# A two-layer diffusion transformer on one NeuronCore: how the end of layer two puts the residual, the last expert product and the final norm together

## The reference, cut to what matters

```python
def grouped_moe(h, router_w, router_bias, w1, w3, w2):
    ...
    for e in range(N_EXPERTS):
        he = (jax.nn.silu(h @ w1[e]) * (h @ w3[e])) @ w2[e]
        out = out + combine[:, e:e + 1] * he
    return out
...
        y = grouped_moe(tokens, router_w, router_bias, w1[l], w3[l], w2[l])
        x = x + mod[:, 5, None] * y[:B * S].reshape(B, S, D)
...
    return rmsnorm(x, g_final)     # x * rsqrt(mean(x*x) + EPS) * g_final
```

## Time and profile before

| | us |
|---|---|
| median of 3 runs | 1107.58 |
| lowest and highest run | 1102.73, 1112.13 |
| the profiled execution: span from the first to the last instruction | 1110.9 |

### The profile page before, as it was taken

The page is one execution under the profiler, slowest core; times in us unless marked ns, Lnnn a source line. Parts: engine busy times, 40 slices in busy tenths (PEclk is TensorE's granted clock), DMA queues, the critical chain, the costliest instruction groups (busy, mean ns, idle before and its releaser), DMA issues.

```text
span 1110.9 us, 24073 instructions
## 1 busy us (share of the span) xinstructions
PE 938.8 (85%) x9092; PEld 539.8 (49%) x9092; DVE 487.4 (44%) x1186; ACT 245.9 (22%) x485; POOL 192.7 (17%) x325
## 2 busy tenths in 40 slices
PE   3999999979986489999978699999798579967695
PEld 2536445555445255656634366543545335544353
DVE  2179336465664434443433576406642612221233
ACT  2100112343322122222222031113421112111121
POOL 4100000110020134443433320000100111110011
PEclk9999999999998689999988899999998689998898
DMA  9997612780003979999999998317802999999993
GB/s 344 396 398 269 263 73 76 216 362 1 1 1 148 379 297 398 418 413 412 414 415 403 369 357 335 110 44 260 335 1 95 374 368 418 412 401 420 410 416 149
DMA packets 58208, 315.75 MB, mean 284 GB/s; under 512 B 6909, under 2 KB 12229, under 8 KB 39169
## 3 DMA queue, kind: packets, MB, share of 16 engines
q1 hardware_dynamic: 47776, 292.17, 66.0%
q0 software_dynamic: 8336, 17.71, 4.4%
q10 hardware_dynamic: 2000, 4.47, 1.0%
HBM read 308.42 MB, written 11.60 MB: 288 GB/s over the span
## 4 chain that ended last, share of the span: by engine, by line
PE 53%; DMA 33%; DVE 5%; issue 4%; DVEq 2%; ACT 1%; SPq 1%; POOL 1%; ACTq 0%; POOLq 0%
PE ps L2011 49%; DMA ring<-in_w 17%; DMA area<-in_w 7%; DMA HT<-in_w 3%; DMA ring<-in_w_in 2%; DMA cst<-in_w 2%; PE ps L2295 2%; DMA area<-in_cst 1%; DMA XG<-in_w 1%; PE ps L2141 1%; DMA area<-h_rows,area 1%; DMA expert_rows<-area 1%; PE ps L2120 1%; PE ps L2320 0%; PE ps L2331 0%
## 5 line engine op out<-in xcount | busy, mean ns | idle before, releaser
L2011 PE MATMUL ps<-ring,area 128*32 128x256 f32 x3520 | 217.8, 400 | 45.9 <-issue 19.6
L2011 PE MATMUL ps<-ring,HT 128*128 128x512 f32 (+1 forms) x576 | 253.0, 591 | 2.3 <-issue 1.8
L2011 PE MATMUL ps<-area 128*32 128x256 f32 (+6 forms) x2072 | 179.4, 396 | 20.1 <-DVE area L1857 10.1
L2011 PEld LDWEIGHTS ps<-ring,area 128*32 128x32 f32 x3520 | 125.0, 115 | 135.2 <-issue 57.3
L2011 PEld LDWEIGHTS ps<-ring,HT 128*128 128x128 f32 x576 | 108.0, 193 | 126.1 <-issue 123.8
L2011 PEld LDWEIGHTS ps<-area 128*32 128x32 f32 (+4 forms) x2072 | 107.6, 147 | 70.0 <-issue 37.7
L1903 DVE STREAM_TRANSPOSE area<-area 128x256 f32<-128x256 f32 x63 | 28.1, 446 | 180.6 <-PE ps L2011 171.2
L2011 PE MATMUL ps<-HT,ring 128*128 128x256 f32 (+1 forms) x320 | 87.6, 432 | 3.5 <-DMA ring<-in_w_in 3.4
L994 POOL DMA_INDIRECT area<-h_rows,area x66 | 69.8, 1057 | 105.4 <-DVEq L1875 43.1
L2011 PEld LDWEIGHTS ps<-HT,ring 128*128 128x128 f32 x320 | 60.8, 193 | 24.9 <-issue 15.0
L1463 DVE SCALAR_TENSOR_TENSOR area<-area,CW 128x512 f32<-128x512 f32 (+1 forms) x120 | 68.8, 614 | 4.5 <-issue 0.5
(11 more groups left out here) (248 smaller groups left out, 900.6 us busy)
## 6 DMA issues: line engine op xcount, KB each, us to landing
ring<-in_w SPq DMA_DIRECT2D x56, 2048.0 KB
ring<-in_w_ada SPq DMA_DIRECT2D x24, 2048.0 KB
ring<-in_w_in SPq DMA_DIRECT2D x10, 2048.0 KB
area<-in_w SPq DMA_DIRECT2D x20, 1024.0 KB
HT<-in_w SPq DMA_DIRECT2D x8, 2048.0 KB
area<-in_w SPq DMA_DIRECT2D x8, 2048.0 KB
late<-in_w SPq DMA_DIRECT2D x8, 1536.0 KB
ring<-in_w_out SPq DMA_DIRECT2D x4, 2048.0 KB
```

The lines of the kernel that those rows point to most:

```text
L2011: return t_.matmul(out, lhsT, rhs, start=first, stop=last_)
```

## The change

It has four parts. First, in layer two PE adds the residual X into the sum banks right after it zeroes them: eight matmuls of the identity with X, one for each tile and column quarter. Second, the last down product goes into bank 1 (`B_END`), is issued before `add_rows(b)`, waits only for `gT`, and both `add_rows` follow it; its rows and one-hot have buffers of their own. Third, in every DVE step, in both layers, `gT` is made before `ym` and `oht`, as soon as the wait for the former down product has passed. Fourth, the end works by halves of the columns: ACT squares the sum banks directly (banks 0 and 1 of the sums, then 2 and 3, two tiles each), DVE meanwhile multiplies the other half with g_final into X, POOL puts the two half sums together and makes both tiles' roots in one go, then DVE scales tile 0 and half of tile 1, ACT the other half, and three stores follow.

```diff
@@ -546,6 +546,8 @@
         YL = cut(TILES * D, U7_AT).rearrange("p (t d) -> p t d", t=TILES)
         YA = [YL[:, 0], YL[:, 1], gate[:, 0], gate[:, 1]]
         YB = [YL[:, 2], YL[:, 3], area[:, 7 * D // 2:9 * D // 2], area[:, HTR_AT + D:HTR_AT + 2 * D]]
+        oht_end, ym_end = G0[0], ym[:, NW:2 * NW]
+        B_END = 1
         GFIN = area[:, AW - NW - D:AW - NW]
         G4 = area[:, AW - NW:AW]
         SQ = [area[:, c:c + D] for c in range(HTR_AT, HTR_AT + TILES * D, D)]
@@ -864,7 +866,9 @@
                         if n != ahead or k:
                             sp.dma_start(piece, src[:, row:row + piece.shape[1]]).then_inc(ring_full[x], 16)
                         row += piece.shape[1]
-            sp.wait_ge(fin_o, 3)
+            sp.wait_ge(fin_o, 1)
+            sp.dma_start(out_v[:, 0], X[:, 0]).then_inc(stored, 16)
+            sp.wait_ge(fin_o, 2)
             sp.dma_start(out_v[:, 1, 0:D // 2], X[:, 1, 0:D // 2]).then_inc(stored, 16)
 
 
@@ -1016,9 +1020,12 @@
                         for r in range(2):
                             gather(2 * i + r, r, pool.snap(made) + r)
                         pool.reg_add(made, made, 2)
-                    for i in range(nq):
-                        pool.wait_ge(ss_done, TILES * (l + 1) + i + 1)
-                        rsqrt(rstd[:, i:i + 1], ss[:, i:i + 1], ms[:, i:i + 1], D).then_inc(rs_done, 1)
+                    pool.wait_ge(ss_done, TILES * DEPTH + 1)
+                    link(g.tensor_scalar(ms[:, 2:4], ss[:, 0:2], 1.0 / D, EPS, ALU.mult, ALU.add))
+                    pool.wait_ge(ss_done, TILES * DEPTH + 2)
+                    link(g.tensor_scalar(ms[:, 0:2], ss[:, 2:4], 1.0 / D, None, ALU.mult))
+                    link(g.tensor_tensor(ms[:, 0:2], ms[:, 0:2], ms[:, 2:4], ALU.add))
+                    g.tensor_tensor(rstd[:, 0:2], ms[:, 0:2], half[:].to_broadcast([P, 2]), ALU.pow).then_inc(rs_done, 1)
                     barrier(pool, bar(l, 6))
                     return
                 pool.wait_ge(y_zero, 64)
@@ -1257,11 +1264,17 @@
                     with act.Fori(0, blocks) as b:
                         act.wait_ge(w13_full[l], b + 1)
                         s.activation(sg, ps[:, B_W13, 0:P], ACT.Silu).then_inc(si_rdy[l], 1)
-                    for i in range(2):
-                        third(l, i)
-                    act.wait_ge(fin_o, 2)
-                    act.dma_start(out_v[:, 0], X[:, 0]).then_inc(stored, 16)
-                    act.wait_ge(fin_o, 4)
+                    act.wait_ge(sums_full, l + 1)
+                    for h in range(2):
+                        if h == 1:
+                            act.wait_ge(comb[l], 1)
+                        for i in range(2):
+                            last = s.activation(SQ[i][:, h * CHUNK:(h + 1) * CHUNK].rearrange("p (j n) -> p j n", j=2), ps[:, B_SUM + 2 * h:B_SUM + 2 * h + 2, i * NW:(i + 1) * NW], ACT.Square,
+                                                accum_out=ss[:, 2 * h + i:2 * h + i + 1])
+                        last.then_inc(ss_done, 1)
+                    act.wait_ge(rs_done, TILES * DEPTH + 1)
+                    s.activation(X[:, 1, CHUNK:D], X[:, 1, CHUNK:D], ACT.Identity, scale=rstd[:, 1:2]).then_inc(comb[l], 1)
+                    act.wait_ge(comb[l], 3)
                     act.dma_start(out_v[:, 1, D // 2:D], X[:, 1, D // 2:D]).then_inc(stored, 16)
                     act.wait_ge(stored, 48)
                     barrier(act, bar(l, 6))
@@ -1914,7 +1927,7 @@
                     v.tensor_copy(xs, xg[:, bass.ds(at_, NW)])
                     dve.drain().then_inc(xs_rdy[l], 1)
 
-                def copy_y(m, summed=False):
+                def product_made(m):
 
                     if l < DEPTH - 1:
                         v.tensor_scalar(gb, G0[0], of_cond[0][:, bass.ds(m, 1)], None, ALU.mult)
@@ -1922,6 +1935,16 @@
                         v.scalar_tensor_tensor(gb, G0[1], of_cond[1][:, bass.ds(m, 1)], gb, ALU.mult, ALU.add)
                         dve.drain()
                     hold(dve, w2_full[l], m + 1, dve_passed)
+
+                def last_rows(m):
+
+                    v.tensor_scalar(oht_end, ROWS1, TK[:, bass.ds(m, 1)], None, ALU.is_equal)
+                    hold(dve, w2_full[l], m + 1, dve_passed)
+                    v.tensor_tensor(ym_end, ps[:, B_END, 0:NW], G4, ALU.mult)
+                    dve.drain().then_inc(y_rdy[l], 1)
+
+                def copy_y(m, summed=False):
+
                     if l == DEPTH - 1:
                         v.tensor_scalar(oht, ROWS1, TK[:, bass.ds(m, 1)], None, ALU.is_equal)
                         v.tensor_tensor(ym[:, 0:NW], ps[:, B_W2, 0:NW], G4, ALU.mult)
@@ -1948,9 +1971,11 @@
                     hold(dve, si_rdy[l], b + 1, dve_passed)
                     v.scalar_tensor_tensor(gg, sg, TW[:, bass.ds(b, 1)], ps[:, B_W13, P:2 * P], ALU.mult, ALU.mult).then_inc(g_rdy[l], 1)
                     if not isinstance(b, int) or b:
-                        copy_y(b - 1 if m is None else m, m is not None)
+                        product_made(b - 1 if m is None else m)
                     dve.drain()
                     v.transpose(gT, gg).then_inc(gt_rdy[l], 1)
+                    if not isinstance(b, int) or b:
+                        copy_y(b - 1 if m is None else m, m is not None)
                     copy_x(b + 2)
 
                 wait_made(dve, ("x0", l))
@@ -1976,18 +2001,25 @@
                     with dve.Fori(PEEL, blocks) as b:
                         step(b)
                         dve.reg_add(copied, copied, 1)
-                copy_y(dve.snap(copied), l < DEPTH - 1)
                 if l == DEPTH - 1:
+                    last_rows(dve.snap(copied))
+                    dve.wait_ge(fin_g, 16)
                     dve.wait_ge(sums_full, l + 1)
-                    for i in range(nq):
-                        add_sums(l, i)
-                    dve.wait_ge(fin_g, 16)
-                    for i in range(2):
-                        dve.wait_ge(rs_done, TILES * DEPTH + i + 1)
-                        for half in (slice(0, D // 2), slice(D // 2, D)):
-                            v.scalar_tensor_tensor(X[:, i, half], X[:, i, half], rstd[:, i:i + 1], GFIN[:, half], ALU.mult, ALU.mult).then_inc(fin_o, 1)
+                    for h in (1, 0):
+                        if h == 0:
+                            dve.wait_ge(ss_done, TILES * DEPTH + 1)
+                        cols = slice(h * CHUNK, (h + 1) * CHUNK)
+                        v.tensor_tensor(X[:, 0:2, cols].rearrange("p i (j n) -> p i j n", j=2),
+                                        ps[:, B_SUM + 2 * h:B_SUM + 2 * h + 2, :].rearrange("p j (i n) -> p i j n", i=2),
+                                        GFIN[:, cols].rearrange("p (j n) -> p j n", j=2).unsqueeze(1).to_broadcast([P, 2, 2, NW]), ALU.mult)
+                        dve.drain().then_inc(comb[l], 1)
+                    dve.wait_ge(rs_done, TILES * DEPTH + 1)
+                    v.tensor_scalar(X[:, 0], X[:, 0], rstd[:, 0:1], None, ALU.mult).then_inc(fin_o, 1)
+                    v.tensor_scalar(X[:, 1, 0:CHUNK], X[:, 1, 0:CHUNK], rstd[:, 1:2], None, ALU.mult).then_inc(fin_o, 1)
                     barrier(dve, bar(l, 6))
                     return
+                product_made(dve.snap(copied))
+                copy_y(dve.snap(copied), True)
                 dve.drain().then_inc(y_rdy[l], 1)
                 dve.drain().then_inc(phase, 1)
                 for i in range(2):
@@ -2379,7 +2411,10 @@
                 for j in range(NG):
                     claim(pe, ("sum", l, j))
                     rows = slice(SLOT * j, SLOT * (j + 1))
-                    made(mm(ps[:, B_SUM + j], cst[rows, C_ZERO:C_ZERO + P], cst[rows, C_I16:C_I16 + CHUNK], True, False), ("sum", l, j))
+                    last = mm(ps[:, B_SUM + j], cst[rows, C_ZERO:C_ZERO + P], cst[rows, C_I16:C_I16 + CHUNK], True, False)
+                    for i in range(S_LAT // P if l == DEPTH - 1 else 0):
+                        last = mm(ps[:, B_SUM + j, i * NW:(i + 1) * NW], ident, X[:, i, j * NW:(j + 1) * NW], False, False)
+                    made(last, ("sum", l, j))
 
                 def add_rows(b, stop=False):
 
@@ -2387,23 +2422,28 @@
                     for i in range(S_LAT // P):
                         for j in range(NG):
                             rows = slice(SLOT * j, SLOT * (j + 1))
-                            last = mm(ps[:, B_SUM + j, i * NW:(i + 1) * NW], oht[rows, i * P:(i + 1) * P], (ymx if l < DEPTH - 1 else ym)[rows, 0:NW], False, stop and i == S_LAT // P - 1)
+                            if l == DEPTH - 1:
+                                lhsT, rhs = (oht_end, ym_end) if stop else (oht, ym[:, 0:NW])
+                            else:
+                                lhsT, rhs = oht, ymx
+                            last = mm(ps[:, B_SUM + j, i * NW:(i + 1) * NW], lhsT[rows, i * P:(i + 1) * P], rhs[rows], False, stop and i == S_LAT // P - 1)
```

(16 more changed lines are left out.)

## The result

The changed kernel takes 1116.64 us in the median (1104.91 to 1125.67, 11 runs), the kernel before 1110.51 in the same comparison (1102.73 to 1114.52, 11 runs): ratio 1.0069, 95% interval 1.0041 to 1.0097. The ratio is the recorded one of the comparison and not the quotient of the two medians, which lie 6.1 us apart; the run of 1125.67 belongs to the slow state and is left out of it. By the ratio the change costs about 7.7 us (4.5 to 10.8), where 0.6 us of gain was forecast. The profiled execution took 1119.82 us with a span of 1117.9; the kernel before had 1110.9.

What follows compares the result with a forecast made beforehand. Layer two's experts were taken as bound by the weight stream, then PE's backlog, then a relay of single steps. Terms -1.4 (end), +0.4 (residual) and +0.4 (gT order) gave -0.6, so 1107.0 us from 1107.58; range 1102 to 1112.

Steps and rivals of the forecast that it cites:

- the residual on PE: Start of layer two's experts: residual matmuls take 3.5 us at full clock, unit 11 issued 2.9 later, cost 0.4 us.
- a sign of being wrong: Start of layer two's sums: residual records at 0.43 us each would show the prediction wrong; 0.22 was expected.
- rival A: Weight stream of layer two: the whole 2.9 us lag passes to the weights, total +1.9, 1109.5 us; chance 0.2.
- rival D: Start of layer two or loops: banks make an engine wait or reordering uncovers one; 1113 us or more; chance 0.05.
- The product tail: End of layer two, last down product and both add_rows: sums there 1.6 us earlier, bounds 0.6 to 2.4.
- the sum's 5.0 us: Product tail: forecast time from the end of the former down product to the end of the last add_rows.
- Rival C: Product tail: DVE late, PE waits 1 us; POOL takes another 0.5; tail -0.1, total +0.7, 1108.3; chance 0.15.
- the norm: End of layer two, from the sums to the first store: 5.15 us against 4.97, bounds 4.3 and 5.9.
- From the sums to the first store: End of layer two, squares, POOL's root and scaling: 5.15 us against 4.97, a loss of 0.2.
- Store to end: End of the kernel: 4.56 us kept, set by the first store's start plus the time of 1 MB.
- gT ahead of ym: DVE steps in both layers: rows come one transpose later, costing 0.4 us at the end of layer one.
- rival B: Start of layer two's experts: PE's clock stays up, the lag vanishes; -1.0, or -1.8 and 1105.8 us; chance 0.15.

Runs made afterwards that it cites:

- the grouped kernel: The changed kernel with the four zeroing matmuls first, then the eight residual matmuls; 1108.96 us, ratio 0.9973 to the kernel before.
- the kernel before, padded: The kernel before with only 64 semaphore increments added ahead of the routing matmuls, where PE is idle; one run, no ratio, product tail 11.3 us.
- the grouped, padded kernel: The changed kernel with zeroing first, residual after, plus 64 semaphore increments ahead of the routing matmuls; 1107.54 us, ratio 0.9965 to the kernel before.

## Why the prediction was wrong

The step that failed is the residual on PE: "Zeroing and residual are 2.1 + 7.0 us of work at 1.2 GHz; 2.1 of it is done by 886.3, the remaining 7.0 takes 3.5 at 2.4". Both halves of it are wrong for the code as it stands. The 2.1 us of zeroing is the time of four matmuls side by side, each on 32 rows of its own; alternated with matmuls over all rows, each takes 2.0. And the clock was taken from the kernel before, where it rose near 886.3; it doesn't rise here. Zeroing and residual took 16.0 us at 1.2 GHz, half of it each, where 5.6 was reckoned; a record of the residual took 0.50, beyond the 0.43 named as a sign of being wrong. Unit 11 came 14.5 us later and not 2.9: 14.0 by the start of the sums, 1.4 by the first up product at the lower clock (5.23 for 3.83), less 0.9 by PE's shorter pause behind it (1.25 for 2.16). With the matmuls grouped, the step's numbers came out nearly (2.09 and 3.82, unit 11 issued 2.7 us later where 2.9 was reckoned, stream full), so the price of the residual was right within 0.3 us and its arrangement, which I had read only for the number of matmuls, was not. That the clock rises late is shown; why it does stays open.

The rest of that part carried: SP waits for that home, the weight stream has no slack, and the loss is the distance of two issues less what is in flight, (904.05 - 887.32) - 5.1 = 11.6 us by the formula, 10.8 by the landing. That is rival A, to which I gave 0.2 and 2.9 us; its bound of 6.4 took half clock but not the zeroing. The median lies where I had put rival D, but what D named, a bank that makes an engine wait or a wait in the loop, isn't what the runs show.

The product tail was right in its mechanism and gained 0.5 instead of 1.6, since a load of code, which the kernel before hid behind its second wait for DVE, became the last to come. It appears in the earlier trace rows only as 2.04 for 32 records instead of 1.93. With the border moved the sum's 5.0 us is what was measured, by two errors of some 0.4 us that cancel. Rival C had PE wait 1 us again, which is near the 1.2 us between the 28th and the 29th record; its cause (DVE late) was wrong, as DVE had the rows ready in time, and its 0.5 us for POOL didn't come. Two sums of this part were also wrong as written: its bounds of 0.6 to 2.4 us of gain and of 4.3 to 5.9 us for the norm add up to +0.3 and -3.1, not to -0.1 and -2.6, and C's own parts make +0.1 for the tail, not -0.1. Neither reaches the size of the miss.

From the sums to the first store I had 5.15 and measured 4.95: POOL's three operations and hand-overs took 1.3 (root of two columns 0.73, estimate 0.72). Store to end 4.56, measured 4.57, as the end set by the first store and 1 MB would have it.

gT ahead of ym was forecast to cost 0.4 at the end of layer one and gained 0.45. Between the down product and DVE's first operation on the rows it was 1.37 us, and is now 0.93 with the transpose inside. In the code, waits for the scatters stand there; that the transpose now runs beside them is my reading and is not shown by itself. The clock of rival B: in the grouped kernel the fall is spared, as the Trainium skill's "TensorE: Matmul & The Clock Gate", Part 1, would have it; in the changed kernel PE was busy for 19 us at 1.2 GHz before it rose, which the same rule, read by busy time, doesn't foresee. The added work need not be the reason for what was spared: in the kernel before, padded, without any residual, the second up product came after 1.93 us of pause and took 3.66 as well.

## What to carry to other kernels

Matmuls on 32 rows each were cheap here only while they stood next to one another: before one puts anything between such matmuls, price each by itself. When a stream of weights bounds a stage, as here, look first at the PE work that stands ahead of a release that the stream's queue waits for; find that release and compare the distance of the two issues with what is in flight. And behind a loop with a length known only on the chip, the first work after the exit can wait for code at a place that any edit ahead of it moves, so a tail's gain has to be looked for again after each edit.

## What the runs showed of the hardware

Four fp32 zeroing matmuls (32 rows, 512 columns) took 2.09 us together on four different groups of rows, 7.19 on the same group, and 2.0 each between full-height ones, all at 1.2 GHz. The Trainium skill, "TensorEngine Tiling (Array Packing)", "The Solution" and "Theoretical Speedup", puts a factor of up to 4 on tiles of 32 rows; the trace agrees, with 3.4.

The granted clock stayed at 1.2 GHz for 19 us in which PE was busy all the time with such single matmuls, with residual ones and with the first up product, and in the one execution with the zeroing on the same rows for the 7 us of zeroing and 5 us on; in the grouped kernel it was at 2.4 GHz 3 us after the zeroing began. Why is not settled by these runs.

A pause of PE behind a loop's exit ended 3.6 to 4.2 us after the loop's last down product in six kernels, with the border 12, 28 or 44 records behind the exit, and 1.9 us after it with the border at 4; 64 instructions moved the border by 32 records. In these seven PE went on 1.3 to 1.5 us after a 16 KB packet on the instruction queue had landed, and the same holds for the pause in the second up product of the grouped, padded kernel. The Trainium skill, "Runtime: NRT & Kernel Launch", "Instruction fetch mechanics", says that a taken branch out of the pages at hand forces a fetch before work goes on; the trace agrees in so far as a load stands behind the loop and work waits for it, and shows what it costs here. That a taken branch set it off, it doesn't show.
